# ScalarE takes two attention units in one group of three, in blocks 3 and 4 of a hybrid attention and expert kernel

## The reference, cut to what matters

```
z = jnp.einsum('bhqd,bhkd->bhqk', q_i, k_i).astype(jnp.float32) * scale
log_fail = jnp.where(mask, -jax.nn.softplus(z), 0.0)
later_fail = lax.cumsum(log_fail, axis=3, reverse=True) - log_fail
w = jnp.where(mask, jnp.exp(jax.nn.log_sigmoid(z) + later_fail), 0.0)
outs.append(jnp.einsum('bhqk,bhkd->bhqd', w.astype(v.dtype), v_i))
```

```
u = expert_u[idx]
act = jax.nn.gelu(jnp.einsum('thkd,td->thk', u, tb).astype(jnp.float32), approximate=False)
coef = (g * act).astype(tb.dtype)
return jnp.einsum('thk,thkd->td', coef, expert_v[idx])
```

## The kernel before, in words

| step | engine, line | group |
|---|---|---|
| scores, first head ahead of the group's L2285, second head behind it | PE L1897 | at(u) |
| logarithms: three activations | ACT L1018, L1019, L1020 | at(u) + 2 |
| softplus | DVE L1312 (L1315 where a mask is needed) | at(u) + 4 |
| sum over later keys ("later") | PE L1903, L1906, L1909 | at(u) + 4 |
| running sum | POOL L873, L875 | at(u) + 8 |
| weights: one exponential | ACT L1063 | at(u) + 5 |
| weights times values ("weigh") | PE L1916 | at(u) + 6 |
| output of a pair of heads, after its last unit | DVE L1350 | two groups after its weights |

## Time and profile before

### The profile page before, as it was taken

One profiled execution on the slowest core, in us unless ns is written; L12 is line 12 of the kernel. 1 busy time (PEld: TensorE's weight loads), 2 busy tenths in 40 slices (PEclk: granted clock), 3 DMA queues, 4 the chain that ended last, 5 costly groups with the idle time before them and its releaser, 6 DMA issues.

```text
span 2903.7 us, 32738 instructions
## 1 busy us (share of the span) xinstructions
PE 2349.3 (81%) x9955; PEld 1049.4 (36%) x9955; DVE 2214.9 (76%) x5454; ACT 1253.3 (43%) x3127; POOL 1363.3 (47%) x1126
## 2 busy tenths in 40 slices
PE   9988888788887888867887788868756779977897
PEld 7564532345333453313421242213311233333332
DVE  4189886786767877679788869878788756899845
ACT  3523377432653235633475447834332432322223
POOL 0024354444554445544565455655555544444442
PEclk9999999999999999979898898978977889987899
DMA  8279999999999999999999999999999999999998
GB/s 317 100 314 413 382 412 419 402 416 389 407 383 416 409 402 404 392 420 420 421 414 418 349 389 382 377 404 391 412 401 402 387 412 413 393 421 386 420 420 347
DMA packets 199519, 1130.54 MB, mean 389 GB/s; under 512 B 29735, under 2 KB 51431, under 8 KB 73719
## 3 DMA queue, kind: packets, MB, share of 16 engines
q0 software_dynamic: 147456, 1026.06, 87.0%
q1 hardware_dynamic: 51888, 102.38, 9.4%
HBM read 1158.08 MB, written 18.02 MB: 405 GB/s over the span
## 4 chain that ended last, share of the span: by engine, by line
PE 37%; DVE 24%; DMA 18%; ACT 11%; issue 8%; POOL 2%; ACTq 0%; POOLq 0%; DVEq 0%; SPq 0%
DMA r_uv<-in_experts,r_wk 18%; PE ps L2285 15%; DVE r_uv L1759 8%; PE ps L1887 4%; PE ps L2069 3%; PE ps L2188 3%; PE ps L2166 2%; ACT L1214 2%; ACT r_uv L1226 2%; PE ps L1881 2%; PE ps L2033 1%; DVE r_wk L1417 1%; DVE r_wk L1419 1%; DVE r_wk L1420 1%; ACT L951 1%
## 5 line engine op out<-in xcount | busy, mean ns | idle before, releaser
L2285 PE MATMUL ps<-r_uv 128*64 128x512 f32 x4096 | 1167.2, 700 | 526.6 <-ACT r_uv L1226 523.0
L930 POOL DMA_INDIRECT r_uv<-in_experts,r_wk x640 | 771.5, 1205 | 920.8 <-PE ps L2285 776.2
L1759 DVE CUSTOM_DVE_ANT_0 r_uv<-r_uv,hnrep 128x1024 f32<-128x1024 f32 x640 | 782.9, 1242 | 312.4 <-DMA r_uv<-in_experts,r_wk 307.3
L2285 PEld LDWEIGHTS ps<-r_uv 128*64 128x64 f32 x4096 | 280.6, 151 | 1173.0 <-ACT r_uv L1226 703.9
L925 POOL DMA_INDIRECT r_uv<-in_experts,r_wk x384 | 494.8, 1289 | 437.6 <-PE ps L2285 314.8
L1214 ACT ACTIVATE r_wk<-r_wk 128x2 f32<-128x2 f32 x512 | 103.8, 203 | 1286.9 <-DVE r_wk L1759 1285.1
L1759 DVE CUSTOM_DVE_ANT_0 stream_chunk<-r_uv,hnrep 128x1024 f32<-128x1024 f32 x192 | 238.5, 1242 | 88.7 <-DMA r_uv<-in_experts,r_wk 88.5
L1759 DVE CUSTOM_DVE_ANT_0 stage<-r_uv,hnrep 128x1024 f32<-128x1024 f32 x192 | 236.0, 1229 | 60.8 <-DMA r_uv<-in_experts,r_wk 57.1
L1226 ACT ACTIVATE r_uv<-cst,r_wk 128x64 f32<-128x64 f32 x634 | 186.0, 340 | 10.3
L1214 ACT ACT_TABLE_LOAD x135 | 173.2, 1283 | 2.4
L951 ACT ACT_TABLE_LOAD x115 | 147.5, 1283 | 12.1 <-PE ps L2146 8.1
(11 more groups left out here) (236 smaller groups left out, 2776.9 us busy)
## 6 DMA issues: line engine op xcount, KB each, us to landing
r_uv<-in_experts,r_wk POOLq DMA_INDIRECT x1024, 11.3
stream_chunk<-in_w_chunks SPq DMA_DIRECT2D x30, 512.0 KB, 8.1
r_wk<-lkv_dram SPq DMA_DIRECT2D x36, 256.0 KB, 8.2
r_wo<-in_dense_u SPq DMA_DIRECT2D x16, 512.0 KB, 7.9
r_wo<-in_experts SPq DMA_DIRECT2D x16, 512.0 KB, 8.0
r_uv<-in_x SPq DMA_DIRECT2D x8, 512.0 KB, 10.7
r_wo<-in_w_chunks SPq DMA_DIRECT2D x8, 512.0 KB, 11.5
r_wk<-in_x SPq DMA_DIRECT2D x8, 512.0 KB, 7.8
```

Of the source, the lines that this page charges most:

```text
L930: g.indirect_dma_start(uv[:, SLOT[G], :], None, experts, bass.IndirectOffsetOnAxis(idx[b % 2][:, k:k + 1], 0)).then_inc(rows_in[SLOT[G]], 16)
L1759: v.tensor_tensor_reduce(spent[k % 2] if b in DENSE else uv[:, slot, 0:D], uv[:, slot, 0:D], hnrep[:, k % GRP, :], 1.0, 0.0, ALU.mult, ALU ...
L2285: last = t_.matmul(ps[HALF * j:HALF * j + HALF, i, :], uv[:, slot, 0:HALF], uv[:, slot, D + 512 * i:D + 512 * i + 512], start=n == 0, stop ...
```

## The change

In blocks 3 and 4 alone, ACT's logarithms and weights of the even units move one group later, so that they stand in the same group as those of the odd unit behind them. Groups 1 modulo 3 (31, 34, 37, ... 58) now take the weights of two units and then the logarithms of two; groups 0 and 2 have no attention work on ACT. PE's weigh of the even units moves one group later too (35, 38, ...), as does DVE's output of the first pair of heads (group 47 to 48). Since scores are held a group longer, a fifth bank (7) joins the four, and the first unit in it waits for the same thing as unit 3. Scores, softplus, later and running sum stay where they were.

```diff
+LATE_BANKS = {0: Z_BANKS, 1: Z_BANKS, 3: Z_BANKS + (7,)}
...
+def logs_at(first, u):
+
+    return LATE_AT[first][u] + LOGS + (first == 3 and u % 2 == 0)
+
+
+def weights_at(first, u):
+
+    return LATE_AT[first][u] + WEIGHTS[first] + (first == 3 and u % 2 == 0)
...
+            def late_bank(first, u, r, c0):
+
+                return grid(ps[0:r, LATE_BANKS[first][u % len(LATE_BANKS[first])], :], 2)[:, :, c0:GW]
...
-                    if late is not None and (late_units(late, n - WEIGHTS[late]) or late_units(late, n - LOGS)):
+                    if late is not None and (units_at(weights_at, late, n) or units_at(logs_at, late, n)):
                         log_exp_table()
-                        for u in late_units(late, n - WEIGHTS[late]):
+                        for u in units_at(weights_at, late, n):
                             late_weights(b, late, u)
-                        for u in late_units(late, n - LOGS):
+                        for u in units_at(logs_at, late, n):
                             late_logs(b, late, u)
...
-                            if n == LATE_AT[late][last_of(late, i)] + WEIGHTS[late] + 2:
+                            if n == weights_at(late, last_of(late, i)) + 2:
                                 late_out(b, late, i)
...
-                    if u < ZB:
+                    zb = len(LATE_BANKS[first])
+                    if u < zb:
 
                         semaphore, value = ((key_kept, 4 * b + 6), (qT_kept, 2 * b + 3), (qT_kept, 2 * b + 4),
-                                            (key_kept, 4 * b + 8))[u]
+                                            (key_kept, 4 * b + 8), (key_kept, 4 * b + 8))[u]
...
-                    if u >= ZB:
-
-                        gate(pe, "pe", lw_ready, ub + u - ZB + 1)
+                    if u >= zb:
+
+                        gate(pe, "pe", lw_ready, ub + u - zb + 1)
...
-                        for u in late_units(late, n - WEIGHTS[late] - 1):
+                        for u in units_at(weights_at, late, n - 1):
                             late_weigh(b, late, u)
```

More of the change, by code:

```diff
@@ L135, in loads_of, with units_at @@
     return sum(2 - (u1 - u0) for u0, u1 in LATE_LOADS[f][m:loads:LKB])
+def logs_at(first, u):
+    return LATE_AT[first][u] + LOGS + (first == 3 and u % 2 == 0)
+def weights_at(first, u):
+    return LATE_AT[first][u] + WEIGHTS[first] + (first == 3 and u % 2 == 0)
+def units_at(at, first, group):
+    return [u for u in range(len(LATE_AT[first])) if at(first, u) == group]
 def late_units(first, group):
@@ L1053, in late_logs @@
                 act.wait_ge(lz_ready, ub + u + 1)
-                unit_logs(u, lsp3[u % 3][0:r, :, c0:GW], bank(u, r, c0))
+                unit_logs(u, lsp3[u % 3][0:r, :, c0:GW], late_bank(first, u, r, c0))
             def late_weights(b, first, u):
@@ L1062, in late_weights @@
                 act.wait_ge(ltri_done, ub + u + 1)
-                a.activation(lw[u % 2][0:r, :, c0:GW], bank(u, r, c0), ACT.Exp).then_inc(lw_ready, 1)
+                a.activation(lw[u % 2][0:r, :, c0:GW], late_bank(first, u, r, c0), ACT.Exp).then_inc(lw_ready, 1)
             def tile_step(step, t):
@@ L1344, in late_softplus @@
                 dve.wait_ge(llog_ready, unit_base(b, first) + u + 1)
-                softplus(u, sp, sp[:, :, c0:GW], bank(u, r, c0), c0, own_)
+                softplus(u, sp, sp[:, :, c0:GW], late_bank(first, u, r, c0), c0, own_)
             def late_out(b, first, i):
@@ L1892, in bank, with late_bank, unit_scores, unit_later @@
                 return grid(ps[r0:r0 + r, Z_BANKS[u % ZB], :], 2)[:, :, c0:c1]
-            def unit_scores(u, h, opens, r, c0, k, q, r0=0):
+            def late_bank(first, u, r, c0, c1=GW):
+                return grid(ps[0:r, LATE_BANKS[first][u % len(LATE_BANKS[first])], :], 2)[:, :, c0:c1]
+            def unit_scores(u, h, opens, into, c0, r, k, q):
                 rows = slice(HD * h, HD * h + HD)
-                t_.matmul(bank(u, r, c0, r0=r0)[:, h, :], k[rows, 0:r], q[rows, c0:GW], start=opens, stop=False,
+                t_.matmul(into[:, h, :], k[rows, 0:r], q[rows, c0:GW], start=opens, stop=False,
                           skip_group_check=True).then_inc(lz_half if opens else lz_ready, 1)
-            def unit_later(u, r, c0, own, sp, acc):
+            def unit_later(into, r, c0, own, sp, acc):
                 rest = c0 + own
-                last = t_.matmul(bank(u, r, c0), negtri[0:r, 0:r], sp[0:r, :, c0:GW], start=False,
+                last = t_.matmul(into(c0, GW), negtri[0:r, 0:r], sp[0:r, :, c0:GW], start=False,
                                  stop=not own and rest == GW, skip_group_check=True)
                 if own:
-                    last = t_.matmul(bank(u, r, c0, rest), ident, maskneg.unsqueeze(1).to_broadcast([P, 2, P]),
+                    last = t_.matmul(into(c0, rest), ident, maskneg.unsqueeze(1).to_broadcast([P, 2, P]),
                                      start=False, stop=rest == GW, skip_group_check=True)
                 if rest < GW:
-                    last = t_.matmul(bank(u, r, rest), negones[:, 0:r], acc[:, :, rest:GW], start=False, stop=True,
+                    last = t_.matmul(into(rest, GW), negones[:, 0:r], acc[:, :, rest:GW], start=False, stop=True,
                                      skip_group_check=True)
@@ L1941, in first_later @@
                     gate(pe, "pe", lacc_ready, sum(x < NT for _, x in FIRST_UNITS[:u - 1]))
-                unit_later(u, r, c0, own, lsp[:, u % 2, :, :], facc[:, p % 2, :, :])
+                unit_later(lambda c0, c1: bank(u, r, c0, c1), r, c0, own, lsp[:, u % 2, :, :], facc[:, p % 2, :, :])
             def first_later_metas(u):
@@ L2005, in late_later @@
                     gate(pe, "pe", lacc_ready, add_base(b, first) + sum(x < NT for _, x in units[:u]))
-                unit_later(u, r, c0, own, lsp3[u % 3], lacc)
+                unit_later(lambda c0, c1: late_bank(first, u, r, c0, c1), r, c0, own, lsp3[u % 3], lacc)
             def late_weigh(b, first, u):
```

6 lines of the change are left out of this document (4 added, 2 removed).

## The result

The changed kernel is slower: 2945.09 us (median of 7 runs, 2926.92 to 2951.65) against 2909.09 us (median of 7, 2905.36 to 2917.47) on the same chip. The ratio is 1.0111, with an interval of 1.0090 to 1.0132. Of 2909 us that is +32 us (26 to 38); the medians lie 36.0 us apart.

A forecast was written before the change was run, and what follows sets the result against it. Beside the DMAs, a circle of waits through ACT and PE was taken as the limit; 9.8 us in block 3, 14.0 in block 4 and 4 for the output copy gave +27.8 us, so 2934 us, range 2906 to 2948.

The forecast's parts named there:

- Table loads: ACT, blocks 3 and 4: 40 loads fewer, 51.3 us; a period's 12 us of busy time become 9.5 us.
- The circle, 15.78 us: ACT and PE waiting for each other, blocks 3 and 4: 15.78 us per three groups at full clock, against 14.24 before.
- In nearly every group: Sign of being right: ACT idle ahead of the odd weights, waiting for PE's later, in nearly every group 1 modulo 3.
- The clock: TensorE's clock falls after PE's 3.1 us idle time: 1.24 us a period added, so 17.02 us a period.
- I take three of four: Share of periods in blocks 3 and 4 taken to have a fallen clock, at 1.65 us each.
- The output copy, +4 us: Block 3, group 48: the copy waits for PE's weigh directly ahead of the pick; 21.2 us instead of 17.0, once.
- Parts at nothing: Fifth bank, moved weigh and even softplus in blocks 3 and 4: no cost counted for them in the sum.
- The moved weigh: Releases two key loads a group later; 8.2 us loads still fit, or PE's scores wait under 1 us.
- The sum: Both blocks: 9.8 us in block 3, 14.0 in block 4 and 4 for the copy, +27.8 us.
- Circle at full clock: Rival: PE's idle time does not bring its clock down; some 2915 us, chance 0.14.
- Hidden: Rival: gathers run ahead, DMAs stay at their limit and the stretches keep their time; 2905 us, chance 0.14.
- Faster: Rival: odd later is ready before ACT asks, the circle does not close, ACT's shorter work counts; 2895 us, chance 0.06.

The follow-up runs named there:

- e9: The changed kernel with ACT's logarithms ahead of the weights and block 3's fourth pick in group 46 instead of 48: 2916.08 us, ratio 1.0007.
- e2: The changed kernel with PE making the opening scores of odd units four times more, ahead of its wait: 2936.37 us, ratio 1.0090.
- e1: The changed kernel with ACT taking the two sets of logarithms ahead of the two weights: 2922.53 us, ratio 1.0038.
- e5: The changed kernel with block 3's fourth pick on DVE moved from group 48 to 46: 2931.55 us, ratio 1.0083.
- e8: The changed kernel with logarithms ahead of weights, DVE's even softplus one group later and block 3's fourth pick in group 46: 2919.85 us, ratio 1.0026.
- e3: The kernel before with the fifth bank and nothing else moved: 2911.35 us, ratio 0.9993.
- e11: The changed kernel without the fifth bank, with the four banks of before: 2942.06 us, ratio 1.0090.
- e4: The kernel before with ACT's logarithms ahead of the weights in each group of blocks 3 and 4: 2910.43 us, ratio 1.0004.
- e10: The kernel before with ACT's logarithms ahead of the weights in each group of blocks 0 to 4: 2907.82 us, ratio 0.9988.
- e6: The changed kernel with PE's weigh of both units, and the first output copy, one group later: 2968.11 us, ratio 1.0191.

## Why the prediction was right

The direction, the place and the mechanism were right. 2934 us were forecast and 2945.09 us measured, inside the range. By its own steps:

- *Table loads.* 51.3 us of ACT in blocks 3 and 4 were to go; ACT has 53.1 us less in all, and a period's 12 us became 8.8 to 9.6 in 14 of 16. As forecast. They are worth nothing that the runs show: e9 keeps this gain and is at 1.0007.
- *The circle, 15.78 us.* Right. The two periods of e2 at full clock that end in the wait for PE measured 15.50 and 15.72 us, and its parts hold in the changed kernel (6.40 us on ACT for 6.53; idle time of 3.10 us for 3.1). The one period there at full clock, 16.08 us, ended behind DVE and is no measure of it. e1 shows the cause, logarithms behind the odd weights. "In nearly every group" was too much: 12 of 16 periods end in the wait.
- *The clock.* The step that was mis-sized is "I take three of four". One period in 16 ran at a granted clock of 1.00 (2.4 GHz throughout), where seven did before; in the other 15 part of the time was at 1.2 GHz. The reading behind it was off as well: before, the waits ahead of L2285 in this place were 0.55 to 3.27 us, not 1.5 to 3.3; behind the three under 1.5 us the clock held, behind nine of the other 13 the product took longer than its 1.94 us. In the changed kernel the 16 waits are 2.64 to 5.09 us, and 15 of them end in a slower product. Without the one at full clock and the one at group 48, 14 periods average 17.60 us, (106.42 + 140.04) / 14, against 17.43 us forecast for a fallen clock and 17.02 us for the mean. In block 4 the eight came to 140.04 us for 136.2, which is 3.8 us too few. The forecast's upper bound for all periods (139.4 us) was nearly the value.
- *The output copy, +4 us.* Right in kind, too small. 24.44 us came for 21.2. Until the pick starts 13.64 us passed (1519.33 to 1532.97) for 11.3: the sum had used durations at full clock for L2314 and the later, in a period that comes just when the clock has fallen (0.81). The second dot product took 2.28 us instead of 1.2, another 1.0. Measured by e5, e9 and e8 the collision is worth 6 to 9 us, not 4. In the trace of e5 the period is 6.6 us shorter and block 3 as a whole 10.5 us (346.0 for 356.5), so it seems to cost the periods beside it too; no run shows that by itself.
- *Parts at nothing.* The fifth bank: confirmed both ways (e3, e11). The moved weigh: its key loads took 9.0 us for 8.2, and scores waited 1.61 us for one in the long period, a little more than the "under 1 us" allowed. The softplus: waits came that the forecast had not seen, 22.4 and 23.8 us, since the odd weights' own wait stands ahead of the logarithms; in 12 periods no cost of theirs shows, by the argument above, and in the one of 16.08 us they are in the chain.
- *The sum.* 27.8 us forecast; the two stretches are 38.4 us longer (20.6 + 17.9), the two blocks 33.4 us, the runs 32 us by their ratio. That the forecast comes so near the runs owes something to luck: the stretches are 10.6 us longer than it said, and no term of it stood for what came next. Some of the loss in block 4's stretch is given back behind it, where the transfers again set the pace and the block as a whole grew by 13.4 us only.

The rivals: *Circle at full clock* fell (granted clock 0.86 and 0.87). *Hidden* fell (DMA share 0.93 and 0.91), but it fits the kernel before, as e4 and e10 show, and e9 (DMA share 0.99 and 0.95). *Faster* fell at the point named for it, the wait ahead of the odd weights (20.9 us in block 4). The Trainium skill's rule in "ScalarE: Activation LUTs", Rules for kernel authors, to group functions by table set, was followed by the change, and here the change cost 32 us through the order and place of other work; with the order mended and the pick moved (e9) it gave nothing that the runs show. The drain that the Trainium skill puts beside a load ("ScalarE: Activation LUTs", What ACT_TABLE_LOAD costs) is not in this trace either: the load at 1832.30 us ends at 1833.58 and the gelu starts at 1833.60.

## What to carry to other kernels

Before work is merged to save a fixed cost on an engine that is 43% busy, find the circle of waits that it stands in and sum that circle for the new order; the engine's own busy time did not tell the outcome here. In a merged group, put what waits for another engine last and what waits for nothing first: the same instructions cost 21 us in the one order and not in the other. When a step is moved later, look at every semaphore that its instructions raise, buffers coming free included (e6 lost 24 us more by those overlooked), and at what now stands beside it on each engine, since one copy ahead of a pick was worth 6 to 9 us.

## What the runs showed of the hardware beyond the forecast

The clock fell behind short idle times of PE, and not always. It fell after a wait of 3.10 us in the changed kernel and after 1.06 us in e2 (3.36 us for the eight matmuls), and it held after 3.27 us in the kernel before. In e2 two waits of 1.59 us, one period apart and behind the same work of PE, ended one with 1.94 us and one with 3.53 us for the same eight matmuls. With the extra matmuls in the idle time the clock stayed at 1.00 in three of the seven periods of block 4 that have them. What decides between the two is not settled by these runs.
